# Expert w2 loads begun by ScalarE after the expert's first product, in a streaming transformer block on one core

## The chip, the cores and the metric

The kernel runs on one core of a Trainium2 chip. The metric is the device time of one execution in microseconds (us). It is given as the median of three runs.

## The reference

One block of a hybrid encoder over 256 tokens of width 1024, in float32: RMSNorm, one input projection, sparse attention with an indexer, a pooling mixer, gates, an output projection, and a mixture of 32 experts of which each token uses 4. The part that matters here is the last:

```python
def _moe(h, router_w, router_b, w1, b1, w2, b2):      # w1 (32, 1024, 2048), w2 (32, 1024, 1024), float32
    tok = h.reshape(-1, D_)                             # 256 tokens
    logits = tok @ router_w + router_b
    topv, topi = lax.top_k(logits, 4)
    topw = jax.nn.softmax(topv, axis=-1)
    combine = sum(one_hot(topi, 32) * topw[..., None], axis=1)
    for e in range(32):
        gu = tok @ w1[e] + b1[e]
        gate = jnp.minimum(gu[:, :1024], 7.0)
        lin = jnp.clip(gu[:, 1024:], -7.0, 7.0)
        act = (lin + 1) * gate * jax.nn.sigmoid(1.702 * gate)
        out = out + combine[:, e:e + 1] * (act @ w2[e] + b2[e])
```

The weights of one expert are 8 MB (w1) and 4 MB (w2); all 32 are read once from HBM.

## The kernel before, in words

The kernel is written engine by engine, with semaphores by hand, so each engine's order is the order of its code.

**The ring.** The experts' weights pass through a ring of 10 slots in SBUF. A slot holds a chunk of 2048 KB (128 partitions of 4096 float32). w1 of an expert is 4 chunks and w2 is 2, so an expert is 6 chunks and the whole is 192. `w1_chunk` and `w2_chunk` number them in the order w1(0), w1(1), w2(0), w1(2), w2(1), w1(3), w2(2), and so on to w1(31), w2(30), w2(31). Chunk n lies in the slot that chunk n - 10 had.

**Who loads.** SP (SyncE) begins every one of these loads in its own queue, one after the other, in the order of the numbers (`load_w1`, line 404, and `load_w2`, line 408). Before each it waits until the slot is free (`slot_free`): until TensorE has used chunk n - 10. That is the semaphore `gemm1` for an expert's last w1 chunk, `gemm2` for its last w2 chunk, and `chunk_used` for the others. The two chunks of w2(e) take the slots of the first two chunks of w1(e), and w1(e+2) takes those of the last two chunks of w1(e) and of both chunks of w2(e-1). The last chunk of all is loaded in two halves (lines 450 and 451).

**What TensorE does for an expert.** In the loop over e: `up_expert(e+1)` is the first product of expert e+1, with the bias (line 309) and 4 chunks of 16 matmuls (line 319), each chunk behind a wait for its landing. Its last matmul raises `gemm1` to e+2. Then come the gather of the rows of expert e+2 (line 280), `down_expert(e)`, which is the second product of expert e (2 chunks of 16 matmuls, line 334, which raises `gemm2`), the transposes of the activations of e+1 (325) and of the rows of e+2 (296), the scatter of e's result to the tokens (343), and the transposes of the put matrix (301). So w2(e) is first used after the whole first product of expert e+1.

**What ScalarE does for an expert.** The sigmoid (`sigmoid_gate(e+1)`, line 652, which waits for VectorE's clamp at line 870 and through it for `gemm1`), the copy of the gathered rows (`rows_out(e+2)`, 656), the copy of the second product (`out_out(e)`, 668), and two more copies (660, 664). It begins a few small loads in its own queue, all before the experts.

Of the kernel before, what the change touches and what calls it, by code (L numbers as in the profile page):

```python
# [41 lines left out]
def block_kernel(nc, x, attn_norm_g, w_in, q_norm_g, k_norm_g, pool_w, pool_b, pool_scale,  # L42
                 w_branch_attn, w_branch_pool, w_out, ffn_norm_g, router_w, router_b,
                 expert_w1, expert_b1, expert_w2, expert_b2, out):
    _, T, D = x.shape
    HD = q_norm_g.shape[1]
    DA = w_branch_attn.shape[1]
    H = DA // HD
    G = len(POOL_WINDOWS)
    E = router_w.shape[2]  # L50
# [23 lines left out]
    RING = 10  # L74
    CHUNK_N = 4096
    W1_ROWS, W2_ROWS = CHUNK_N // (2 * FE), CHUNK_N // D
    W1_CHUNKS, W2_CHUNKS = KD // W1_ROWS, KD // W2_ROWS
# [3 lines left out]
    with ExitStack() as ctx:  # L81
# [3 lines left out]
        def sem(name):  # L85
            return ctx.enter_context(nc.semaphore(name))
# [5 lines left out]
        def scratch(slot, at, size):  # L92
# [89 lines left out]
        chunk_in = [sem(f"chunk_in{i}") for i in range(RING)]  # L182
# [12 lines left out]
        pick_ok, gathered, hTe_ok, gemm1, gate_ok, sig_ok, half_ok, glu_ok = (  # L195
            sem(n) for n in "pick_ok gathered hTe_ok gemm1 gate_ok sig_ok half_ok glu_ok".split())
# [46 lines left out]
        def w1_chunk(e, c):  # L243

            return c if e == 0 else W1_CHUNKS + (e - 1) * (W1_CHUNKS + W2_CHUNKS) + c

        def w2_chunk(e, c):

            return (e + 1) * (W1_CHUNKS + W2_CHUNKS) + (W1_CHUNKS - W2_CHUNKS if e < E - 1 else -W2_CHUNKS) + c
# [4 lines left out]
        def chunk_slot(n):  # L254
            return ring[:, SLOT_ORDER[n % RING], :]
# [8 lines left out]
        def w2_dram(e, c):  # L264
            rows = W2_ROWS * P
            return expert_w2[0][bass.ds(e, 1), c * rows:(c + 1) * rows, :].rearrange("a (p k) n -> p (a k n)", p=P)
# [107 lines left out]
        def _(sp):  # L374
# [27 lines left out]
            def load_w1(e, c):  # L402
                n = w1_chunk(e, c)
                sp.dma_start(chunk_slot(n), w1_dram(e, c)).then_inc(chunk_in[n % RING], 16)

            def load_w2(e, c):
                n = w2_chunk(e, c)
                sp.dma_start(chunk_slot(n), w2_dram(e, c)).then_inc(chunk_in[n % RING], 16)
# [21 lines left out]
            def slot_free(n):  # L430
                if n in W1_LAST:
                    sp.wait_ge(gemm1, W1_LAST.index(n) + 1)
                elif n in W2_LAST:
                    sp.wait_ge(gemm2, W2_LAST.index(n) + 1)
                else:
                    sp.wait_ge(chunk_used, n + 1 - sum(last < n for last in W1_LAST + W2_LAST))

            for e in range(1, E):
                if e < E - 1:
                    for c in range(W1_CHUNKS):  # L440
                        slot_free(w1_chunk(e + 1, c) - RING)
                        load_w1(e + 1, c)
                for c in range(W2_CHUNKS):
                    slot_free(w2_chunk(e, c) - RING)
                    if (e, c) != (E - 1, W2_CHUNKS - 1):
                        load_w2(e, c)
                        continue
                    n, half = w2_chunk(e, c), CHUNK_N // 2
                    src = w2_dram(e, c)
                    sp.dma_start(chunk_slot(n)[:, 0:half], src[:, 0:half]).then_inc(chunk_in[n % RING], 16)  # L450
                    sp.dma_start(chunk_slot(n)[:, half:CHUNK_N], src[:, half:CHUNK_N]).then_inc(tail_in, 16)
# [56 lines left out]
        def _(act):  # L508
# [141 lines left out]
            def sigmoid_gate(e):  # L650
                act.wait_ge(gate_ok, e + 1)
                nc.scalar.activation(sig_e, gate_e, ACT.Sigmoid, scale=SWIGLU_ALPHA).then_inc(sig_ok, 1)  # L652

            def rows_out(e):
                act.wait_ge(gathered, e)
                nc.scalar.copy(rows_e, ps_gather[:, :]).then_inc(rows_ok, 1)

            def actT_out(e):
                act.wait_ge(actT_ps, e + 1)
                nc.scalar.copy(actT_e, ps_gate[:, :]).then_inc(actT_sb, 1)  # L660

            def putT_out(e):
                act.wait_ge(put_ps, e + 1)
                nc.scalar.copy(putT[:, :], ps_out[:, 0:T]).then_inc(put_sb, 1)

            def out_out(e):
                act.wait_ge(gemm2, e + 1)
                nc.scalar.copy(out_e, ps_out[:, :]).then_inc(out_ok, 1)  # L668
# [5 lines left out]
            for e in range(E - 1):  # L674
                sigmoid_gate(e + 1)
                if e + 2 < E:
                    rows_out(e + 2)
                out_out(e)
                actT_out(e + 1)
                putT_out(e + 1)  # L680
            out_out(E - 1)

            act.wait_ge(s["most_ok"], 1)
# [638 lines left out]
```

## Time and profile before

| | us |
|---|---|
| median of three runs (1145.51 to 1148.51) | 1147.47 |
| the profiled execution's own time | 1149.56 |
| its span, first to last instruction | 1147.8 |
| TensorE busy | 1095.4 (95%) |
| ScalarE busy | 141.5 (12%) |
| issue to landing of a chunk, median | 42.0 |

The span is divided into 40 slices of 28.7 us. The experts begin at about 223 us, with the eighth slice. A busy digit is a share in tenths, and "PEclk" is the clock that was granted to TensorE. For the DMA engines the page gives the share in which the core's 16 engines were busy and the GB/s that they moved. A chunk is 2.097 MB.

### The profile page before, as it was taken

What the parts mean: (1) busy time and instruction counts of PE and PEld (TensorE: products, weight loads), DVE (VectorE), ACT (ScalarE), POOL (GpSimd) and SP (SyncE); (2) the same over time, 40 slices, a digit from 0 to 9 for tenths busy, and PEclk for the clock granted to TensorE, in tenths of its full rate; (3) what the DMA queues carried; (4) which work ended last, traced back from release to release, by engine and by line L of the source; (5) the groups of instructions that cost most, each with busy time, mean ns of one, the idle gap of its engine ahead of it and who ended that gap; (6) DMA issues with size and microseconds to landing.
All of it is one profiled execution on the core that took longest, in us unless ns stands there. A gap on an engine that the chain in (4) does not pass through costs nothing.

```text
span 1147.8 us, 11145 instructions
## 1 busy us (share of the span) xinstructions
PE 1095.4 (95%) x4910; PEld 427.0 (37%) x4910; DVE 197.1 (17%) x498; ACT 141.5 (12%) x287; POOL 15.1 (1%) x35
## 2 busy tenths in 40 slices
PE   7999999999999999999999998999999999999996
PEld 5464544633333333333333332333333333333332
DVE  1630011411111121111111111111111111111111
ACT  2114111310000110001010000000000000000001
POOL 0004000000000000000000000000000000000000
PEclk9999999789999999999999999999999999999999
DMA  9824527579999999999999999999999999999995
GB/s 344 321 101 147 219 74 286 232 305 426 429 428 427 427 428 429 427 426 428 428 427 429 428 428 427 427 428 427 427 428 427 429 428 428 428 428 428 426 428 227
DMA packets 41667, 432.81 MB, mean 377 GB/s; under 512 B 4189, under 2 KB 5745, under 8 KB 16913
## 3 DMA queue, kind: packets, MB, share of 16 engines
q1 hardware_dynamic: 40128, 431.26, 89.8%
q10 hardware_dynamic: 1488, 0.82, 0.3%
q8 instruction: 40, 0.66, 0.2%
q14 instruction: 11, 0.08, 0.0%
HBM read 431.01 MB, written 1.05 MB: 376 GB/s over the span
## 4 chain that ended last, share of the span: by engine, by line
PE 68%; DMA 31%; DVE 0%; issue 0%; ACT 0%; ACTq 0%
DMA ring<-in_expert_w_dram 31%; PE bank L319 25%; PE bank L334 12%; PE bank L955 8%; PE bank L343 4%; PE bank L280 2%; PE bank L1111 2%; PE bank L1091 2%; PE bank L309 2%; PE bank L325 1%; PE bank L1016 1%; PE bank L296 1%; PE bank L301 1%; PE bank L945 1%; PE bank L289 1%; PE bank L1038 0%
## 5 line engine op out<-in xcount | busy, mean ns | idle before, releaser
L319 PE MATMUL bank<-ring,work 128*64 128x512 f32 x2048 | 454.0, 598 | 17.8 <-DMA ring<-in_expert_w_dram 17.1
L319 PEld LDWEIGHTS bank<-ring,work 128*64 128x64 f32 x2048 | 143.4, 138 | 326.4 <-issue 285.9
L334 PE MATMUL bank<-ring,work 128*64 128x512 f32 x1024 | 230.5, 598 | 19.4 <-DMA ring<-in_expert_w_dram 18.9
L334 PEld LDWEIGHTS bank<-ring,work 128*64 128x64 f32 x1024 | 73.2, 137 | 171.0 <-issue 137.3
L870 DVE TENSOR_SCALAR work<-bank 128x512 f32<-128x512 f32 x32 | 22.1, 692 | 485.7 <-PE bank L319 468.5
L955 PE MATMUL bank<-ring 128*128 128x512 f32 x224 | 98.5, 594 | 0.0
L652 ACT ACTIVATE work<-work 128x512 f32<-128x512 f32 x32 | 20.2, 630 | 499.8 <-DVE work L870 499.8
L343 PE MATMUL bank<-work,putT 64*128 64x512 f32 x256 | 63.6, 615 | 0.7 <-ACT work L668 0.7
L365 DVE TENSOR_TENSOR work<-bank,vecs 128x512 f32<-128x512 f32 x32 | 22.1, 692 | 232.8 <-PE bank L296 230.8
L955 PEld LDWEIGHTS bank<-ring 128*128 128x128 f32 x224 | 41.8, 190 | 48.4 <-issue 48.2
L280 PE MATMUL bank<-xn,pick 128*64 128x512 f32 x248 | 58.5, 592 | 0.0
L668 ACT COPY work<-bank 128x512 f32<-128x512 f32 x32 | 18.8, 587 | 225.5 <-PE bank L334 225.5
L309 PE MATMUL bank<-b_rows,bias_pick 32*64 32x512 f32 x256 | 35.7, 627 | 0.0
L280 PEld LDWEIGHTS bank<-xn,pick 128*64 128x64 f32 x248 | 17.7, 137 | 35.0 <-issue 35.0
L343 PEld LDWEIGHTS bank<-work,putT 64*128 64x128 f32 x256 | 22.0, 186 | 20.5 <-issue 15.1
L1111 PE MATMUL bank<-ring,xn 128*128 128x512 f32 x64 | 28.4, 593 | 0.0
L325 PEld LDWEIGHTS bank<-ident,work 128*128 128x128 f32 x128 | 18.1, 210 | 26.6 <-issue 26.6
L356 DVE TENSOR_SCALAR put<-slot_id,place,weight 128x128 f32<-128x128 f32 x64 | 19.3, 344 | 38.5 <-PE bank L301 38.5
L325 PE MATMUL bank<-ident,work 128*128 128x128 f32 x128 | 24.3, 314 | 0.0
L874 DVE SCALAR_TENSOR_TENSOR work<-work 128x512 f32<-128x512 f32 x32 | 22.2, 693 | 3.7 <-DVE work L871 0.5
L878 DVE TENSOR_TENSOR work<-work 128x512 f32<-128x512 f32 x32 | 22.2, 692 | 1.4 <-ACT work L652 0.4
L871 DVE TENSOR_SCALAR work<-bank 128x512 f32<-128x512 f32 x32 | 21.8, 681 | 0.0
(181 smaller groups left out, 454.6 us busy)
## 6 DMA issues: line engine op xcount, KB each, us to landing
ring<-in_expert_w_dram SPq DMA_DIRECT2D x191, 2048.0 KB, 42.0
ring<-in_w_in_dram SPq DMA_DIRECT2D x8, 2048.0 KB, 19.9
ring<-in_w_out_dram SPq DMA_DIRECT2D x2, 2048.0 KB, 7.9
ring<-in_w_branch_attn_dram SPq DMA_DIRECT2D x1, 2048.0 KB, 7.9
ring<-in_w_branch_pool_dram SPq DMA_DIRECT2D x1, 2048.0 KB, 7.9
ring<-in_expert_w_dram SPq DMA_DIRECT2D x2, 1024.0 KB, 43.8
ring<-in_w_in_dram SPq DMA_DIRECT2D x1, 1296.0 KB, 8.1
xs<-in_x_dram SPq DMA_DIRECT2D x2, 512.0 KB, 4.5
```

The lines of the kernel that those rows point to most:

```text
L280: mm = pe.matmul(ps_gather[SLOTS * half:SLOTS * (half + 1), :], pick[:, tt, :], xn[:, tt, half * BANK:(half + 1) * BANK], start=(tt == 0), ...
L309: mm = pe.matmul(dst, bias_pick[rows, :], b1_rows[rows, :], start=first, stop=not first, skip_group_check=True)
L319: mm = pe.matmul(dst, hTe[:, at:at + SLOTS], w[:, col:col + BANK], start=(k == 0 and not bias_first), stop=(k == KD - 1 and bias_first), s ...
L325: mm = pe.transpose(ps_gate[:, j * P:(j + 1) * P], every(act_e, W2_ROWS, j), ident[:, :])
L334: mm = pe.matmul(ps_out[SLOTS * half:SLOTS * (half + 1), :], actT_e[:, at:at + SLOTS], w[:, col:col + BANK], start=(k == 0), stop=(k == KD ...
L343: mm = pe.matmul(acc[2 * tt + half][:, :], putT[rows, tt * P:(tt + 1) * P], out_e[rows, :], start=False, stop=True, skip_group_check=True)
L365: return nc.vector.tensor_tensor(hTe.rearrange("p (j h n) -> p j h n", j=4, h=2), ps_gather[:, :].rearrange("p (j h n) -> p j h n", j=4, h ...
L874: nc.vector.scalar_tensor_tensor(out=lin_e, in0=lin_e, scalar=1.0, in1=gate_e, op0=ALU.add, op1=ALU.mult).then_inc(half_ok, 1)
L878: nc.vector.tensor_tensor(act_e, lin_e, sig_e, ALU.mult).then_inc(glu_ok, 1)
L955: mm = pe.matmul(dst, hT[:, k, tt * P:(tt + 1) * P], w[:, k, :], start=(k == 0), stop=(k == KD - 1))
L1091: mm = pe.matmul(bank[2 + 2 * (j % 2) + n][:, :], src[:, k, tt * P:(tt + 1) * P], w[:, k, half * BANK:(half + 1) * BANK], start=(k == 0), ...
L1111: mm = pe.matmul(bank[2 * tt + half][:, :], mergedT[tt][:, k, :], w[:, k % 4, half * BANK:(half + 1) * BANK], start=(k == 0), stop=(k == K ...
```

## The change

SP no longer loads w2 of the experts 1 to 30. ScalarE begins these loads in its own queue: after the sigmoid of expert e+1 it waits for `gemm1` of that expert, which means until all four w1 chunks of e+1 are used, and starts both w2 chunks of e+1. Then it goes on with the copy of the gathered rows. SP still loads all of w1, w2(0) and w2(31). The slots and the chunks' semaphores are the same.

```diff
--- before.py
+++ after.py
@@ -440,7 +440,7 @@
                     for c in range(W1_CHUNKS):
                         slot_free(w1_chunk(e + 1, c) - RING)
                         load_w1(e + 1, c)
-                for c in range(W2_CHUNKS):
+                for c in range(W2_CHUNKS if e == E - 1 else 0):
                     slot_free(w2_chunk(e, c) - RING)
                     if (e, c) != (E - 1, W2_CHUNKS - 1):
                         load_w2(e, c)
@@ -663,6 +663,13 @@
                 act.wait_ge(put_ps, e + 1)
                 nc.scalar.copy(putT[:, :], ps_out[:, 0:T]).then_inc(put_sb, 1)
 
+            def load_w2(e):
+
+                act.wait_ge(gemm1, e + 1)
+                for c in range(W2_CHUNKS):
+                    n = w2_chunk(e, c)
+                    act.dma_start(chunk_slot(n), w2_dram(e, c)).then_inc(chunk_in[n % RING], 16)
+
             def out_out(e):
                 act.wait_ge(gemm2, e + 1)
                 nc.scalar.copy(out_e, ps_out[:, :]).then_inc(out_ok, 1)
@@ -674,6 +681,7 @@
             for e in range(E - 1):
                 sigmoid_gate(e + 1)
                 if e + 2 < E:
+                    load_w2(e + 1)
                     rows_out(e + 2)
                 out_out(e)
                 actT_out(e + 1)
```

SP's queue at the experts 0 and 1, before. Of these rows the `x3` and the `gemm1` behind it are w1(2), the next row is w2(1), the four after it are w1(3), and the last is w2(2):

```order
L408 DMA ring<-in_expert_w2_dram 128x4096
L404 DMA ring<-in_expert_w1_dram 128x4096 [waits chunk_used] x3
L404 DMA ring<-in_expert_w1_dram 128x4096 [waits gemm1]
L408 DMA ring<-in_expert_w2_dram 128x4096 [waits chunk_used] x2
L404 DMA ring<-in_expert_w1_dram 128x4096 [waits chunk_used]
L404 DMA ring<-in_expert_w1_dram 128x4096 [waits gemm1]
L404 DMA ring<-in_expert_w1_dram 128x4096 [waits chunk_used]
L404 DMA ring<-in_expert_w1_dram 128x4096 [waits gemm2]
L408 DMA ring<-in_expert_w2_dram 128x4096 [waits chunk_used] x2
```

The same place now:

```order
L408 DMA ring<-in_expert_w2_dram 128x4096
L404 DMA ring<-in_expert_w1_dram 128x4096 [waits chunk_used] x3
L404 DMA ring<-in_expert_w1_dram 128x4096 [waits gemm1]
L404 DMA ring<-in_expert_w1_dram 128x4096 [waits chunk_used]
L404 DMA ring<-in_expert_w1_dram 128x4096 [waits gemm1]
L404 DMA ring<-in_expert_w1_dram 128x4096 [waits chunk_used]
L404 DMA ring<-in_expert_w1_dram 128x4096 [waits gemm2]
```

After w1(2), SP goes straight to w1(3), whose first chunk waits for the third chunk of w1(1) to be used. Before, the two chunks of w2(1) came between them, behind the first and second chunk of w1(1).

ScalarE's order at expert 1 (first row: its sigmoid), before:

```order
L652 ACTIVATE work<-work 128x512 [waits gate_ok]
L656 COPY work<-bank7 128x512 [waits gathered]
L668 COPY work<-bank6 128x512 [waits gemm2]
L660 COPY work<-bank4 128x512 [waits actT_ps]
L664 COPY putT<-bank6 128x256 [waits put_ps]
```

And now (line 675 is the former 668):

```order
L652 ACTIVATE work<-work 128x512 [waits gate_ok]
L671 DMA ring<-in_expert_w2_dram 128x4096 [waits gemm1]
L671 DMA ring<-in_expert_w2_dram 128x4096
L656 COPY work<-bank7 128x512 [waits gathered]
L675 COPY work<-bank6 128x512 [waits gemm2]
L660 COPY work<-bank4 128x512 [waits actT_ps]
L664 COPY putT<-bank6 128x256 [waits put_ps]
```

The two loads stand between the sigmoid and the copy of the gathered rows.

## Rows read from the trace of the kernel before

**Rows 1.** Page, part 2: TensorE and DMA busy in 40 slices, in tenths.

```profile
PE   7999999999999999999999998999999999999996
DMA  9824527579999999999999999999999999999995
```

**Rows 2.** Stretches: length, busy PE, PEld, DVE, ACT, POOL; then PEclk, DMA share, GB/s.

```profile
10.00:15.00 5.00, 3.72 (x19) 3.20 (x18) 1.15 (x2) 1.83 (x7) 0.00 (x0) 1.00 1.05 387
15.00:20.00 5.00, 5.00 (x25) 4.21 (x24) 0.00 (x0) 0.58 (x1) 0.00 (x0) 1.00 1.07 386
...
235.00:243.00 8.00, 8.00 (x43) 2.36 (x39) 1.79 (x3) 1.68 (x3) 0.00 (x0) 1.00 1.00 430
249.00:256.00 7.00, 7.00 (x29) 1.97 (x29) 1.53 (x5) 0.32 (x1) 0.00 (x0) 0.72 0.29 122
285.00:600.00 315.00, 315.00 (x1522) 111.45 (x1520) 52.06 (x118) 32.78 (x59) 0.00 (x0) 1.00 1.01 428
```

**Rows 3.** Waits from 600 to 1136 us: us in total, times, longest.

```profile
PE bank L334 <- DMA ring<-in_expert_w_dram: 18.9, 17, 2.4
PE bank L319 <- DMA ring<-in_expert_w_dram: 17.1, 17, 1.2
```

**Rows 4.** Timeline of SP's loads, neighbours merged: start, us to the last's end.

```profile
255.86 3.76 SPq L408 DMA_DIRECT2D ring<-in_expert_w_dram  x2
262.73 12.34 SPq L404 DMA_DIRECT2D ring<-in_expert_w_dram  x4
282.79 3.76 SPq L408 DMA_DIRECT2D ring<-in_expert_w_dram  x2
289.65 12.34 SPq L404 DMA_DIRECT2D ring<-in_expert_w_dram  x4
...
1090.76 2.65 SPq L451 DMA_DIRECT2D ring<-in_expert_w_dram  x1
```

**Rows 5.** Issue to landing of the load at 255.86, then of the last.

```profile
DMA to landing us min/median/max: 8.1/8.1/8.1
...
DMA to landing us min/median/max: 44.8/44.8/44.8
```

**Rows 6.** TensorE's timeline: the second product of expert 1 begins.

```profile
294.59 1.89 PE L334 MATMUL bank<-ring,work 128*64 128x512 f32 x8
```

**Rows 7.** TensorE's timeline at the end: start, us, idle before it.

```profile
1116.06 3.65 PE L319 MATMUL bank<-ring,work 128*64 128x512 f32 x16 [1.01 <-DMA ring<-in_expert_w_dram]
1121.05 3.65 PE L334 MATMUL bank<-ring,work 128*64 128x512 f32 x16 [1.34 <-DMA ring<-in_expert_w_dram]
1125.85 3.65 PE L334 MATMUL bank<-ring,work 128*64 128x512 f32 x16 [1.14 <-DMA ring<-in_expert_w_dram]
...
1133.05 7.09 PE L334 MATMUL bank<-ring,work 128*64 128x512 f32 x32 [0.51 <-issue]
1140.82 1.99 PE L343 MATMUL bank<-work,putT 64*128 64x512 f32 x8 [0.68 <-ACT work L668]
```

**Rows 8.** Page, part 6: loads in ScalarE's queue and SP's; KB, us to landing.

```profile
pool_wsb<-in_pool_w_dram ACTq DMA_DIRECT2D x1, 256.0 KB, 11.1
ring<-in_w_in_dram SPq DMA_DIRECT2D x8, 2048.0 KB, 19.9
```

**Rows 9.** ScalarE: a load of its queue, then its work in one expert.

```profile
16.35 0.45 ACTq L540 DMA_DIRECT2D pool_wsb<-in_pool_w_dram  x1
...
854.68 0.63 ACT L652 ACTIVATE work<-work 128x512 f32<-128x512 f32 x1 [16.49 <-DVE work L870]
855.67 0.59 ACT L656 COPY work<-bank 128x512 f32<-128x512 f32 x1 [0.36 <-PE bank L280]
863.76 0.59 ACT L668 COPY work<-bank 128x512 f32<-128x512 f32 x1 [7.50 <-PE bank L334]
```

**Rows 10.** TensorE after its longest wait among the experts, and the clock there.

```profile
713.16 5.35 PE L334 MATMUL bank<-ring,work 128*64 128x512 f32 x16 [2.45 <-DMA ring<-in_expert_w_dram]
...
714.00:719.00 5.00, 5.00 (x18) 1.69 (x15) 0.00 (x0) 0.44 (x1) 0.00 (x0) 0.68 1.03 439
```

## The prediction, made before the changed kernel ran

> **What bounds the kernel now.** I read the two strips of the page first. TensorE is busy nearly everywhere, and so are the DMA engines from the tenth slice on [rows 1]. That both are near full doesn't say which one sets the pace, so the second view is the table of stretches: from 285 us on the DMA engines move 428 GB/s without a gap (a share of 1.01) [rows 2]. A chunk of 2.097 MB thus takes 2.097 / 428 = 4.90 us, and an expert's six take 29.4 us. The third view is SP's timeline. The w2 loads of two experts running begin at 255.86 and 282.79 us, so TensorE, which frees the slots, needs 26.93 us for an expert when it doesn't wait [rows 4]. TensorE is the faster of the two by 2.46 us an expert. It first lives on the chunks that are loaded ahead, and then waits: from 600 us on 18.9 us before chunks of w2 and 17.1 us before chunks of w1 [rows 3]. The DMA stream is the bound. It has run without a break since the load at 255.86 us: that chunk lands 8.1 us after its issue, at 264.0, the other 177 follow at 4.90, which gives 1131, and the last one lands at 1090.76 + 44.8 = 1135.6 us [rows 4, 5]. The 4.3 us between are small gaps of 0.5% in all, which I leave as they are. The end is then set by two things alone: when this stream begins and whether it breaks, and how much TensorE work hangs on its last chunks.
>
> Right before the stream there is a hole. From 249 to 256 us the DMA share is 0.29 [rows 2]: w1(2) is loaded and SP waits for the first chunk of w1(1) to be used.
>
> **The change part by part.**
>
> *The start of the stream.* Before, the hole ends with w2(1) at 255.86 us. Now SP's next load is w1(3,0), which waits for the third chunk of w1(1). In the trace it goes out at 262.73 us [rows 4], and nothing delays TensorE before that, so it will again. ScalarE's w2(1) comes later still, after the fourth chunk. The hole grows by 262.73 - 255.86 = 6.87 us. From 262.73 to about 275 us all six loads of this round are begun; they last 29.4 us, to 292, and the next load (w1(4,0)) goes out at 289.65 us [rows 4]. So the stream does not break again, and each later round has 2.46 us more in hand. The last chunk lands 6.9 us later, at 1142.5 us. **Term 1: +6.9 us.**
>
> Does TensorE feel the hole at once? w2(1) is begun at about 268 us and needed at 294.59 us [rows 6]. At half the rate, two chunks take 4 x 4.90 = 19.6 us and land by about 291 us with the fixed part of 8.1 - 4.90 = 3.2 us. There are 4 us to spare. This costs nothing by itself.
>
> *The order at the end.* Now as the queue stands, four chunks come behind w1(31,3): both of w2(30) and both of w2(31). 1116.06 + 4 x 4.90 = 1135.7 us, which is where the last one lands [rows 5, 7]. With the change w2(30) is begun right after the first product of expert 30. That is one round (29.4 us) before the first product of expert 31 ends. Two queues then want the same engines. If they get half each, w2(30) is in after 19.6 us (and 3.2), before w1(31,3), which it has pushed back. Behind w1(31,3) there is only w2(31), 9.8 us. So w1(31,3) lands at 1142.5 - 9.8 = 1132.7 us instead of 1116.0. This is 6.9 us from term 1, and two chunks' time on top. **Term 2: +9.8 us.** The bytes are the same; what is worse is that the chunk on which most of the remaining TensorE work hangs now comes later in the stream.
>
> *What follows w1(31,3).* Before, it is 1140.82 + 1.99 - 1116.06 = 26.75 us to the end of the scatter, and this holds two waits for w2(30), of 1.34 and 1.14 us [rows 7]. Now w2(30) has landed, and these go. **Term 3: -2.5 us.** What is late next? The second product of expert 31 then starts 1133.05 - 1116.06 - 2.48 = 14.5 us behind 1132.7, at 1147.2 us, when w2(31) has been in for almost 5 us. Nothing else takes their place.
>
> *The middle.* The stream stays the bound: 29.4 us against 26.93. The waits of 36 us move to another place, one wait of about 2.5 us an expert at the last w1 chunks, none at w2. That alone costs nothing. It has a side effect, though. The longest wait of before, 2.45 us, is followed by 16 matmuls in 5.35 us instead of 3.65, with the granted clock at 0.68 over that stretch, that is, partly at 1.2 GHz instead of 2.4 [rows 7, 10]. If every wait of 2.5 us does this, TensorE needs 26.93 + 1.7 = 28.6 us an expert, still under 29.4, so the middle hides it. Before the last product it is not hidden: 0 to +1.7 us. I take half. **Term 4: +0.8 us.**
>
> *What ScalarE pays.* Two issues of about 0.45 us [rows 9] in each of 30 experts, 27 us in all. They stand between the sigmoid, which ends at 855.31, and the copy of the rows at 855.67 us. Behind that copy ScalarE is idle for 7.50 us, and TensorE wants the copied rows only after the second product, about 7 us later [rows 9, 7]. A copy that is 0.6 us later is covered. SP's last issue took 2.65 us [rows 4]; two of these would make 5 us, still within the 7. Cost 0; what the cover would have to lose is 7 us. SP's 60 fewer issues gain nothing, since SP waits anyway.
>
> *The rate with two queues at once.* No row of before shows two queues full of 2048 KB loads. The nearest are the first loads: 387 GB/s in 10 to 15 us with SP's queue alone, 386 in 15 to 20 us with ScalarE's beside it, in smaller packets [rows 2]. And ScalarE's 256 KB are in after 11.1 us beside SP's queue, whose 2048 KB blocks need 19.9 [rows 8], so one queue doesn't wait for the other to be empty. The gain is bounded by 439 GB/s, the highest figure in any row, over 5 us [rows 10]: 2.5% of the 872 us of stream, -22 us. The same distance down, 417 GB/s, would be +22 us. I take 0, by the nearest row, 386 against 387, and keep about 1% to either side for the range.
>
> The Trainium skill (DMA: Bandwidth & Descriptors, "Issuing engines are not separate DMA queues") says that loads issued by different engines run on the same 16 DMA engines and interleave, and that a second issuer saves only issue time. It speaks against any gain, and by it the sum is the one above. The same page ("Bandwidth") gives 435 GB/s as the ceiling of the fabric; a stream at that figure would be an estimated 1.6% or 14 us shorter, which would just cancel the sum. The trace has 430 GB/s over 8 us of such loads, and 439 only over 5 us [rows 2, 10].
>
> **The sum.** +6.9 + 9.8 - 2.5 + 0.8 = +15.0 us. The span goes from 1147.8 to 1162.8, the profiled execution's time from 1149.56 to 1164.6. That execution lies 2.1 us above the median of 1147.47, so for the median I say 1162.5 us, +1.3%.
>
> **The rivals.**
>
> *A. The stream gets faster with two queues (the other side).* While one queue is between two packets, the other one fills the engine. For it: a granted share of 16 engines says little about gaps inside a packet, and overlap holds in 4 of 6 chunks. Against: 386 beside 387. At 434 GB/s, halfway to the bound of 439, the price is -12, the sum +3, the time 1150; it decides from 4.82 us a chunk on, where the 14 to 15 us are won back. At the bound it is 1141. Chance 0.11.
>
> *B. The engines serve the loads in the order of issue.* Then w2(30) doesn't push ahead. At the end it is issued behind w1(31) and w2(31), and lands last, at 1142.5 us. From the landing of the second w2(30) chunk to the end it was 1140.82 + 1.99 - 1125.85 = 16.96 us [rows 7]: 1159.5 against 1142.8, +16.7, the time 1164. Rows 8 speak against it. Chance 0.08.
>
> *C. The stream gets slower.* Two streams from different places of HBM disturb each other by 1%: +9, the time 1171 (at the bound of 417, 1185). For it: nothing but that it's untried. Chance 0.09.
>
> *D. ScalarE's queue gets less than a third.* Below that, 2 x 4.90 x 3 = 29.4 us is a whole round, and w2 comes late for every second product. At 0.3 it is 32.7 us, 3.3 late, of which 2.5 are idle anyway: 0.8 x 30 = 24, with term 1 some +31, the time 1178. Chance 0.04.
>
> The forecast has the remaining 0.68.
>
> **How the numbers follow.** Against 1147.47, 0.3% is 3.4 us, about what a measurement of this kernel can tell from no change. Faster needs 1144 or less, which only the far end of A gives: 0.04. Same is the middle of A: 0.05. Its near end (1151 to 1155), the forecast and B, C, D are slower: 0.91. The forecast's own range is 1158 to 1166 (term 4, the rate by 0.4%). For 8 in 10 I add B and most of C, and the nearer end of A: 1154 to 1172.
>
> **What would show it.** Right: the hole before the stream ends at about 262.7 us instead of 255.9, with the first ScalarE load near 268; the last chunk lands near 1142 us; the waits for DMA at the second product are gone, and one of 2 to 3 us stands before the last w1 chunk in each later expert; some of them with a lower clock behind; w2 loads land some 20 to 23 us after issue, where all loads needed 42; GB/s stays at 428. Wrong: GB/s of 432 or more (A) or 424 or less (C); waits before the second product (B, D); a hole in the DMA strip past 300 us.

## The result, and the profile after

| | before | changed |
|---|---|---|
| median of 4 runs, us | 1147.99 | 1160.98 |
| lowest to highest | 1145.51 to 1148.52 | 1159.12 to 1161.85 |
| profiled execution's own time | 1149.56 | 1159.12 |
| its span | 1147.8 | 1157.3 |

The ratio is 1.0118, 95% interval 1.0104 to 1.0131: slower by 13 us. A second set, taken later (below), gave 1.0129, 1.01 to 1.0158.

The strips of the changed kernel's page, as in [rows 1]:

```profile
PE   7999999999999999989999999999999989999997
DMA  9823517569999999999999999999999999999993
```

They look like those of before. What differs is too small for a digit of 29 us. The stretches of the changed kernel, with the columns of [rows 2]:

```profile
249.00:256.00 7.00, 7.00 (x34) 2.30 (x32) 0.00 (x0) 0.00 (x0) 0.00 (x0) 1.00 0.06 23
256.00:262.00 6.00, 6.00 (x30) 2.01 (x28) 0.20 (x1) 0.00 (x0) 0.00 (x0) 1.00 0.45 134
...
285.00:600.00 315.00, 304.33 (x1448) 105.95 (x1446) 48.37 (x110) 30.34 (x55) 0.00 (x0) 0.99 1.01 428
600.00:900.00 300.00, 284.50 (x1324) 98.25 (x1322) 46.58 (x105) 28.81 (x52) 0.00 (x0) 0.98 1.01 428
900.00:1100.00 200.00, 189.66 (x888) 65.23 (x886) 28.19 (x67) 18.09 (x33) 0.00 (x0) 0.97 1.01 427
```

From 249 to 256 us the DMA share fell from 0.29 to 0.06: the hole is wider. The figures of this one stretch can't be compared exactly, since w1(2) came in somewhat earlier here (the clock, below); the run that gives w2 of 1 to 3 back to SP measures the hole alone. Behind it stands the same rate of 427 to 428 GB/s, now with two queues. The clock's column goes down from 1.00 to 0.97 towards the end.

The issues around the hole (start, us to the last one's end):

```profile
258.36 3.76 SPq L404 DMA_DIRECT2D ring<-in_expert_w_dram  x2
262.54 0.84 ACTq L671 DMA_DIRECT2D ring<-in_expert_w_dram  x2
```

The last load's second half (duration in ns, start), with the time from issue to landing of both halves:

```profile
L451 SPq DMA_DIRECT2D ring<-in_expert_w_dram x1: 433/433/433, 1103.1 to 1103.1; - x1
DMA to landing us min/median/max: 32.9/34.0/35.0
```

The stream begins at 258.36 us and its last part lands at 1103.1 + 35.0 = 1138.1: 879.7 us. Before it was 1135.6 - 255.86 = 879.7 us [rows 4, 5]. To a tenth of a microsecond the same bytes take the same time.

The groups of loads on the page, with KB and median us to landing, beside the 42.0 of before:

```profile
ring<-in_expert_w_dram SPq DMA_DIRECT2D x131, 2048.0 KB, 36.4
ring<-in_expert_w_dram ACTq DMA_DIRECT2D x60, 2048.0 KB, 19.5
```

The 19.5 us is the middle between two kinds of loads and no load's own time. The two loads of a pair stand one behind the other in ScalarE's queue. Over all 60 of them, and over the first pair, issued at 262.54 and 262.92 us, the times to landing are:

```profile
DMA to landing us min/median/max: 13.7/19.5/25.1
...
DMA to landing us min/median/max: 15.8/20.4/25.1
```

The first load of a pair lands 13.7 to 15.8 us after its issue, the second 23.2 to 25.1 us. The second lands a median of 9.8 us behind the first. That is 2 x 4.90 us for one chunk: half the rate, while SP's queue has the other half. And the waits for loads from 600 to 1136 us, where [rows 3] had two lines:

```profile
PEld bank L319 <- DMA ring<-in_expert_w_dram: 43.3, 18, 4.6
PE bank L319 <- DMA ring<-in_expert_w_dram: 28.0, 17, 3.7
```

The line of the second product (L334) is gone. All waiting is now before w1. The end of TensorE's timeline, to be laid beside [rows 7]:

```profile
1115.63 10.52 PE L319 MATMUL bank<-ring,work 128*64 128x512 f32 x48
1128.36 3.65 PE L319 MATMUL bank<-ring,work 128*64 128x512 f32 x16 [2.21 <-DMA ring<-in_expert_w_dram]
1131.85 7.04 PE L334 MATMUL bank<-ring,work 128*64 128x512 f32 x32
...
1142.43 7.09 PE L334 MATMUL bank<-ring,work 128*64 128x512 f32 x32 [0.51 <-issue]
1150.19 1.99 PE L343 MATMUL bank<-work,putT 64*128 64x512 f32 x8 [0.68 <-ACT work L675]
```

w1(31,3) lands at 1128.4 us, 9.8 us before the last chunk and no longer 19.6. From there to the end of the scatter it is 1150.19 + 1.99 - 1128.36 = 23.8 us without one wait for a load, against 26.75.

The two profiled executions differ by 9.5 us, the medians by 13. The traces show one reason: the clock just before the stream. In the profile of before TensorE began the first product of expert 1 later:

```profile
251.40 4.85 PE L319 MATMUL bank<-ring,work 128*64 128x512 f32 x18
```

In the changed kernel's profile:

```profile
247.80 13.95 PE L319 MATMUL bank<-ring,work 128*64 128x512 f32 x64
```

Before, the clock was at 0.72 over the stretch from 249 to 256 us [rows 2], and here it was at 1.00. What the profiled before lost there, 3.6 us, and the 0.8 us of the product's slower start hide 4.4 of the 6.9 us of the first term in a comparison of the two traces: 258.36 - 255.86 = 2.5 us, and 2.5 + 9.8 - 2.9 = 9.4 us of span. Other executions weren't traced, but among 17 of the kernel before that were timed beside one group of the runs below, the 4 with a mean granted clock of 0.989 over the execution, which the profiled one had too, took 1151.1 to 1151.6 us, and the 13 with 0.993 to 0.996 took 1145.2 to 1148.7 us.

### The profile page after: what moved, and what is told of

Same layout as the page of the kernel before. It is cut to its first block, busy times and chain, and to the rows that moved or that the text cites. A ratio compares the mean times of both kernels' runs of the same rounds, so it can differ in the third digit from the quotient of the medians.

```text
span 1157.3 us, 11145 instructions
## 1 busy us (share of the span) xinstructions
PE 1102.0 (95%) x4910; PEld 428.9 (37%) x4910; DVE 197.0 (17%) x498; ACT 141.3 (12%) x287; POOL 15.1 (1%) x35
## 4 chain that ended last, share of the span: by engine, by line
PE 51%; DMA 48%; DVE 0%; issue 0%; ACT 0%; ACTq 0%
DMA ring<-in_expert_w_dram 48%; PE bank L319 14%; PE bank L334 12%; PE bank L963 8%; PE bank L280 3%; PE bank L1119 2%; PE bank L1099 2%; PE bank L343 1%; PE bank L1024 1%; PE bank L309 1%; PE bank L953 1%; PE bank L289 0%; PE bank L325 0%; PE bank L1046 0%; DMA xs<-in_x_dram 0%; PE bank L942 0%
## 5 line engine op out<-in xcount | busy, mean ns | idle before, releaser
L319 PE MATMUL bank<-ring,work 128*64 128x512 f32 x2048 | 468.7, 613 | 39.5 <-DMA ring<-in_expert_w_dram 38.7
L319 PEld LDWEIGHTS bank<-ring,work 128*64 128x64 f32 x2048 | 145.9, 141 | 358.8 <-issue 297.1
L334 PE MATMUL bank<-ring,work 128*64 128x512 f32 x1024 | 225.2, 592 | 0.5 <-issue 0.5
L334 PEld LDWEIGHTS bank<-ring,work 128*64 128x64 f32 x1024 | 73.7, 137 | 146.1 <-issue 146.1
L675 ACT COPY work<-bank 128x512 f32<-128x512 f32 x32 | 18.7, 586 | 199.4 <-PE bank L334 199.4
## 6 DMA issues: line engine op xcount, KB each, us to landing
ring<-in_expert_w_dram SPq DMA_DIRECT2D x131, 2048.0 KB, 36.4
ring<-in_expert_w_dram ACTq DMA_DIRECT2D x60, 2048.0 KB, 19.5
ring<-in_w_in_dram SPq DMA_DIRECT2D x8, 2048.0 KB, 19.5
```

What stands on the lines that cost most here:

```text
L319: mm = pe.matmul(dst, hTe[:, at:at + SLOTS], w[:, col:col + BANK], start=(k == 0 and not bias_first), stop=(k == KD - 1 and bias_first), s ...
L334: mm = pe.matmul(ps_out[SLOTS * half:SLOTS * (half + 1), :], actT_e[:, at:at + SLOTS], w[:, col:col + BANK], start=(k == 0), stop=(k == KD ...
```

## The experiments

All were timed in three groups, on three chips, each group beside runs of the kernel before on the same chip. The groups are the runs that give back w2 of 1 to 3, of 30, and of both, with the changed kernel again; then w2 of 1 alone, one queue, ScalarE's early issue, and the better kernel; then the two runs over three rounds at the end. Where a number of microseconds against before is given, it is the ratio's distance from 1 times 1147. In the expectations T is the theory of the prediction, with terms 1 to 3. Q blames ScalarE's queue, and C here blames TensorE's clock (it isn't the prediction's rival C).

### Undo the start: SP loads w2 of the experts 1 to 3

```diff
-                for c in range(W2_CHUNKS if e == E - 1 else 0):
+                for c in range(W2_CHUNKS if e <= 3 or e == E - 1 else 0):
...
-                    load_w2(e + 1)
+                    if e + 1 > 3:
+                        load_w2(e + 1)
```

> SP loads w2 of the experts 1 to 3 again, in its old order; ScalarE begins those of 4 to 30. Theory T (the loss is a later start of the stream, +6.9 us, and w2(30) ahead of w1(31), +9.8 - 2.5 us; measured sum +13): the hole at 250 us is as before, and by expert 4 the DMA engines are 3 x 2.46 = 7.4 us behind TensorE, enough to cover the later issue. So the first term goes: +6 us against the kernel before (5 to 8). Rival Q (each load in ScalarE's queue, or two queues at once, costs something, 13 us over 30 experts): 27/30 of it stays, +11.7 us. Rival C (the falls of TensorE's clock cost it): they stay, +13 us.

Measured: 1152.92 us, ratio 1.006 (1.0037 to 1.0084), +6.9 us. The loads of 27 of 30 experts are still ScalarE's and half of the loss is gone. Theory T fits; Q's +11.7 lies outside the interval (4.2 to 9.6 us), and so does C's +13: in the same trace TensorE still waits 30.0 us for loads before w1, and none before w2, and the mean granted clock is 0.982, where the changed kernel's is 0.980 in its trace of the same group.

```profile
PEld bank L319 <- DMA ring<-in_expert_w_dram: 45.0, 17, 4.0
PE bank L319 <- DMA ring<-in_expert_w_dram: 30.0, 17, 3.1
```

The two traces of that group also give term 1 by itself, since TensorE reached this place at the same time in both (w1(1)'s product starts at 247.89 and 247.74 us). The first load behind the hole, here and in the changed kernel:

```profile
251.58 0.33 SPq L408 DMA_DIRECT2D ring<-in_expert_w_dram  x1
...
258.30 0.33 SPq L404 DMA_DIRECT2D ring<-in_expert_w_dram  x1
```

The hole ends 6.7 us later with the change; term 1 says 6.9.

### Undo it for expert 1 alone

```diff
-                for c in range(W2_CHUNKS if e == E - 1 else 0):
+                for c in range(W2_CHUNKS if e == 1 or e == E - 1 else 0):
...
-                    load_w2(e + 1)
+                    if e + 1 > 1:
+                        load_w2(e + 1)
```

> SP loads w2(1) again, ScalarE those of 2 to 30. T: the first stream begins at 255.86 us as before, but its six chunks are through after 29.4 us, and the next load, w1(4,0), goes out only at 289.65 us. A new hole of 289.65 - 255.86 - 29.4 = 4.4 us opens one round later; only 2.5 us of the 6.9 are won back: +10.5 us against the kernel before (9 to 12), with a hole in the DMA share near 290 us. Rival S (only the load at the first hole matters): 6.9 us are won, +6 us.

Measured: 1160.33 us, ratio 1.0106 (1.0083 to 1.0128), +12.2 us, just above the 9 to 12 expected; S's +6 is out (interval 9.5 to 14.7 us). The time alone can't tell this kernel from the changed one; the trace can. The second hole is there. The stretches of this kernel:

```profile
249.00:256.00 7.00, 7.00 (x38) 2.21 (x32) 1.04 (x5) 0.00 (x0) 0.00 (x0) 1.00 0.60 204
256.00:262.00 6.00, 6.00 (x32) 2.01 (x28) 0.00 (x0) 0.00 (x0) 0.00 (x0) 1.00 1.00 429
280.00:290.00 10.00, 10.00 (x48) 3.30 (x46) 0.00 (x0) 0.00 (x0) 0.00 (x0) 1.00 0.63 236
```

The first hole closes early (share 0.60 where the changed kernel has 0.06). But from 280 to 290 us the share is 0.63, a hole of 3.7 us (4.4 expected). From the first issue behind the first hole to the last landing the stream takes 884.4 us in this trace instead of 879.7, so the second hole costs 4.7 us. The hole was moved by one round, and only some 2 us of it were closed.

### Undo the end: SP loads w2(30)

```diff
-                for c in range(W2_CHUNKS if e == E - 1 else 0):
+                for c in range(W2_CHUNKS if e >= E - 2 else 0):
...
-                    load_w2(e + 1)
+                    if e + 1 < E - 2:
+                        load_w2(e + 1)
```

> SP loads w2(30) again, behind w1(31); ScalarE begins those of 1 to 29. T: behind w1(31,3) there are again four chunks, it lands two chunks earlier, and the waits before w2(30) come back: 9.8 - 2.5 = 7.3 us less than the changed kernel, +5 to +7 us against the kernel before. Q: 29/30 stays, +12.6 us. C: +13 us.

Measured: 1158.77 us, ratio 1.01 (1.008 to 1.0119), +11.5 us. This was a miss: T said +5 to +7. Neither do Q (+12.6) and C fall by this run alone. TensorE's timeline of this kernel shows why:

```profile
1101.36 5.35 PE L319 MATMUL bank<-ring,work 128*64 128x512 f32 x16 [2.20 <-DMA ring<-in_expert_w_dram]
...
1119.69 13.95 PE L319 MATMUL bank<-ring,work 128*64 128x512 f32 x64
1133.47 7.04 PE L334 MATMUL bank<-ring,work 128*64 128x512 f32 x32
```

The last wait for a load is at w1(30,3), which had w2(29) ahead of it as in the changed kernel. After that all 64 matmuls of expert 31's first product run through without a wait, so w1(31) had been there in time. It was of no use, because TensorE itself was one reordering late, and it gains only 29.4 - 26.93 = 2.5 us on the loads in a round.

The clock took part of even that. The 16 matmuls behind the wait took 5.35 us instead of 3.65, at a granted clock of 0.72 from 1101 to 1107 us. At the same place the changed kernel's profile has

```profile
1099.00 3.65 PE L319 MATMUL bank<-ring,work 128*64 128x512 f32 x16 [0.58 <-DMA ring<-in_expert_w_dram]
```

From there to the second product of expert 30 it is 1131.85 - 1099.00 = 32.9 us in the changed kernel and 1133.47 - 1101.36 = 32.1 us here: 0.7 us are gained in this profiled execution, about the 2.5 us less 1.7 us for the slow matmuls. No wait follows in which those could hide.

### Both at once, with only expert 30 at the end

SP loads w2 of 1 to 3 and of 30:

```diff
-                for c in range(W2_CHUNKS if e == E - 1 else 0):
+                for c in range(W2_CHUNKS if e <= 3 or e >= E - 2 else 0):
...
-                    load_w2(e + 1)
+                    if 3 < e + 1 < E - 2:
+                        load_w2(e + 1)
```

> Both: SP loads w2 of 1 to 3 and of 30, ScalarE those of 4 to 29. T: both terms go, 0 us against the kernel before (-1.5 to +1.5), though 26 experts still use two queues, the waits still stand before w1, and the clock still falls. Q: 26/30 stays, +11.3 us. C: +13 us less the share of experts with falls that is gone, above +10 us.

Measured: 1150.87 us, ratio 1.003 (1.0017 to 1.0043), +3.4 us. Q and C are out by far: 26 of 30 experts run as in the changed kernel. But T's 0 is missed too (interval 1.9 to 4.9 us). What the run above was short of is about 5 us: the 7.3 us of the end less the 2.5 us that one round gives back, 4.8. Of this 3.4 us show here. In the profile it is 4.8: behind the last landing, at 1130.4 us, the kernel runs 17.0 us to its end, against 12.2 us in the profile of before.

### The changed kernel again, on the same chip

No edit: it gives the size of the loss on the chip of three of the runs above (w2 of 1 to 3, of 30, and both; w2 of 1 alone was timed on another).

> The changed kernel on the same chip as the three others: +13 us (11.5 to 15) against the kernel before, ratio 1.0118 within 0.002, by every theory.

Measured: 1160.49 us, ratio 1.0129 (1.01 to 1.0158), +14.8 us.

### One queue, the same late moment

```diff
+            for c in range(W1_CHUNKS):
+                next_w1(2, c)
+            for e in range(1, E - 1):
+                if e < E - 2:
+                    next_w1(e + 2, 0)
+                    next_w1(e + 2, 1)
...
+                sp.wait_ge(gemm1, e + 1)
+                for c in range(W2_CHUNKS):
+                    load_w2(e, c)
+                if e < E - 2:
+                    next_w1(e + 2, 2)
+                    next_w1(e + 2, 3)
```

(`next_w1` waits for the slot and loads. For expert 30 the two chunks of w2(31) stand in place of w1's, ahead of w2(30); the lines left out do this, and ScalarE begins no expert's load.)

> No load of ScalarE. SP begins w2(e) itself, at the same moment as the changed kernel does (after gemm1 of e), behind w1(e+2,1) and ahead of w1(e+2,2), all in one queue; at the end w2(30) stands behind w2(31). T: the start is late by 6.9 us as in the changed kernel, and in one queue w2(30) now lands last, so that 16.96 us of TensorE work follow the last chunk: 2.5 us more than the changed kernel, +14 to +17 us against the kernel before; w2 lands about 35 us or more after issue instead of 19.5. Q (ScalarE's queue is the cost): the cost goes, 0 to +7 us.

Measured: 1165.45 us, ratio 1.0163 (1.0142 to 1.0184), +18.7 us (16.3 to 21.1), a little over T's range. ScalarE's queue is not what costs: without it the loss is all there, and Q's 0 to +7 is out. In the two profiles the stream begins at 264.31 us here and at 255.86 before, 8.45 us later and 1.6 more than term 1; the clock before it was lower still, 0.60 from 249 to 256 us. w2 loads land after 31.4 us (median), the two of a pair 4.9 us apart instead of 9.8, and the end of TensorE's timeline has the two waits before w2(30) again, behind which all the rest hangs:

```profile
1123.11 13.95 PE L319 MATMUL bank<-ring,work 128*64 128x512 f32 x64
1139.75 3.65 PE L334 MATMUL bank<-ring,work 128*64 128x512 f32 x16 [2.69 <-DMA ring<-in_expert_w_dram]
1144.52 3.65 PE L334 MATMUL bank<-ring,work 128*64 128x512 f32 x16 [1.12 <-DMA ring<-in_expert_w_dram]
```

### ScalarE's queue, the old moment

```diff
             def load_w2(e):
 
-                act.wait_ge(gemm1, e + 1)
                 for c in range(W2_CHUNKS):
                     n = w2_chunk(e, c)
+                    act.wait_ge(chunk_used, n - RING + 1 - sum(last < n - RING for last in W1_LAST + W2_LAST))
...
             for e in range(E - 1):
+                if e + 2 < E:
+                    load_w2(e + 1)
                 sigmoid_gate(e + 1)
                 if e + 2 < E:
-                    load_w2(e + 1)
                     rows_out(e + 2)
```

> ScalarE begins w2 of 1 to 30 in its own queue, but at the moment at which SP did in the kernel before: chunk by chunk, when the slot is free, ahead of the sigmoid. T: the first term goes (no longer hole), the order at the end stays as in the changed kernel or a little earlier: 9.8 - 2.5 = +7.3 us, +6 to +8 us against the kernel before. Q: all 60 loads are in ScalarE's queue, +13 us. A rival S2 (the second queue is harmless and only the late issue costs): 0 us.

Measured: 1155.37 us, ratio 1.0068 (1.0048 to 1.0088), +7.8 us. Both Q (13) and S2 (0) are out. The first issue is at 255.72 us, so the hole is that of before, and what is left is the order at the end. It isn't quite the end that T had in mind. The lines of this profile:

```profile
1099.96 5.02 PE L319 MATMUL bank<-ring,work 128*64 128x512 f32 x16 [4.36 <-DMA ring<-in_expert_w_dram]
...
1117.96 13.95 PE L319 MATMUL bank<-ring,work 128*64 128x512 f32 x64
```

The last wait is before w1(30,3), as in the run with w2(30) given back, and w1(31) is there in time. In the kernel before the same matmuls began at 1086.70 us. Both streams begin within 0.2 us of each other and both end at 1135.6 to 1135.7 us, so w1(30,3) is 13.3 us late by order alone, and TensorE makes up for a part of it. So T's +7.3 fits by its size, and not by the chunk that it named. The second queue isn't harmless, but not because it is a queue: half the rate goes to the loads that aren't due yet.

### Undo the end over three rounds

SP loads w2 of 28 to 30:

```diff
-                for c in range(W2_CHUNKS if e == E - 1 else 0):
+                for c in range(W2_CHUNKS if e >= E - 4 else 0):
...
-                    load_w2(e + 1)
+                    if e + 1 < E - 4:
+                        load_w2(e + 1)
```

> SP loads w2 of the experts 28 to 30, ScalarE those of 1 to 27. The run that gave only w2(30) back to SP kept 11.5 us of the loss, and in its trace the first product of expert 31 ran without any wait for a load: TensorE itself was late there, since w1(30) had still landed behind w2(29), and it wins back only 29.4 - 26.93 = 2.5 us an expert. Theory T, mended: the order has to be undone over three rounds (3 x 2.5 = 7.4 us) for the end to come back. Expected: 9.8 - 2.5 = 7.3 us less than the changed kernel, +5.5 to +7.5 us against the kernel before. Rival Q (cost per load of ScalarE's queue): 27/30 of the loss, about +13 us. Rival E (the order at the end was never worth more than the 2 to 3 us of that run): +11 us.

Measured: 1154.08 us, ratio 1.0049 (1.0032 to 1.0066), +5.6 us. Q and E are out.

### Both, over three rounds each

```diff
-                for c in range(W2_CHUNKS if e == E - 1 else 0):
+                for c in range(W2_CHUNKS if e <= 3 or e >= E - 4 else 0):
...
-                    load_w2(e + 1)
+                    if 3 < e + 1 < E - 4:
+                        load_w2(e + 1)
```

> SP loads w2 of 1 to 3 and 28 to 30, ScalarE those of the 24 experts between, late as in the changed kernel. T, mended: both terms are gone, -1 to +1 us against the kernel before, though the middle is wholly the changed kernel's (two queues, late issues, falls of the clock). Q: 24/30 of the loss, about +11 us. E: +3 us, like the run with only w2(30).

Measured: 1147.84 us, ratio 1.0003 (0.9985 to 1.0021), +0.3 us. 24 of the 30 experts run with the change, and no cost of it is left (interval -1.7 to +2.4 us); E's +3 is out too. The stretch of this kernel from 400 to 900 us, and the end of its TensorE timeline:

```profile
400.00:900.00 500.00, 478.07 (x2247) 165.52 (x2243) 75.03 (x172) 46.95 (x85) 0.00 (x0) 0.98 1.01 427
```

```profile
1104.95 13.95 PE L319 MATMUL bank<-ring,work 128*64 128x512 f32 x64
1118.73 3.60 PE L334 MATMUL bank<-ring,work 128*64 128x512 f32 x16
1122.56 3.65 PE L334 MATMUL bank<-ring,work 128*64 128x512 f32 x16 [0.23 <-DMA ring<-in_expert_w_dram]
```

The clock stays at 0.98 in the middle, as in the changed kernel, at no cost that shows. At the end a wait stands before w2(30) again (0.23 us), the sign that TensorE has just caught up with the loads.

### A better kernel: begin the stream earlier

The same reasoning shortens the hole of the kernel before. It ends when w1(1,0) is used. Ahead of that TensorE runs eight matmuls that start the accumulators with b2.

```diff
-            for j in range(2 * TT):
+            for j in range(0, 2 * TT, 2):
                 start_acc(j)
...
                 if e + 2 < E:
                     gather_expert(e + 2)
+                if e == 0:
+                    for j in range(1, 2 * TT, 2):
+                        start_acc(j)
                 down_expert(e)
```

> The kernel before, all loads in SP's queue, but two of the four groups of matmuls that start the accumulators with b2 (line 1147) run after the first product of expert 1 instead of ahead of it. They are half of 3.7 to 4.4 us. T says that the hole at 250 us ends when the first chunk of w1(1) is used and that the whole stream hangs on it: 1.8 to 2.2 us earlier, -2 us against the kernel before (-3 to -1). A theory in which TensorE's total work or the DMA bytes alone set the time says 0.

Measured: 1144.07 us, ratio 0.9974 (0.996 to 0.9987), -3.0 us, faster than both. Only half of the matmuls can move, since the other half's b2 lies where the activations' transposes of expert 0 go. Its timeline around the place:

```profile
241.67 1.98 PE L1147 MATMUL bank<-work,pool_wsb 32*128 32x512 f32 x4
...
246.12 13.95 PE L319 MATMUL bank<-ring,work 128*64 128x512 f32 x64
259.90 1.89 PE L280 MATMUL bank<-xn,pick 128*64 128x512 f32 x8
261.72 1.98 PE L1147 MATMUL bank<-work,pool_wsb 32*128 32x512 f32 x4
```

TensorE does the same work, 1.98 us of it 20 us later, and the kernel is shorter by 3.0 us (1.5 to 4.6). The first product of expert 1 begins at 246.12 us; in the changed kernel, which has the old order here, it began at 247.80. That is 1.7 us, in two profiles with the full clock at this place. What goes beyond it may be the clock again, which is granted in full from 242 to 262 us here and stood at 0.83 in the profile of before. Whether moving the matmuls also keeps the clock up isn't shown.

## Why the prediction was right

The forecast was 1162.5 us, and 1160.98 was measured. By its steps:

- *The bound.* Right. 879.7 us of stream in both profiles; 427 to 428 GB/s in every long stretch.
- *Term 1, the later start, +6.9.* Right. Giving w2 of 1 to 3 back to SP took 14.8 - 6.9 = 7.9 us off on the same chip, and in the two traces of that group the stream begins 6.7 us apart. In the profiles of before and after only 2.5 us show, since the clock had been low at that place in the profiled before. The prediction's words that nothing delays TensorE before that, so that it will be the same again, were wrong: that clock did. I read the 262.73 us of the first SP load from that one execution; in the changed one it was 258.36. The difference of the two issues (6.87 us, two chunks of matmuls) held, the absolute times did not.
- *Term 2, the order at the end, +9.8, and term 3, -2.5.* Right: 9.8 us from w1(31,3) to the last landing, and 23.8 instead of 26.75 us behind it, so -2.9. Early issue in ScalarE's queue (+7.8) and giving back 28 to 30 (14.8 - 5.6 = 9.2 us off, on two chips) each frame the 7.3 us within their intervals. For the early issue the trace has another chunk late than the one that the term names, w1(30,3) and not w1(31,3). And at most 2.5 us of the 9.8 come back by putting right the last round alone.
- *Term 4, the clock, +0.8.* Half right. The clock does fall behind longer waits in the middle. In the changed kernel's profile, one of those:

```profile
508.53 5.35 PE L319 MATMUL bank<-ring,work 128*64 128x512 f32 x16 [3.69 <-DMA ring<-in_expert_w_dram]
```

  It costs nothing there. It did cost 1.7 us in the run with only w2(30) given back, where it fell behind the last wait of all. At the end of the changed kernel's profile the last 16 matmuls of the first product took 3.65 us, so the term was 0 in the profiled run. This accounts for 0.8 of the 1.5 us by which the forecast was too high, as far as one execution can tell.
- *ScalarE's cost, 0.* Right: two issues in 0.84 us, and none of TensorE's waits is for ScalarE in the middle.
- *The rate with two queues, 0.* Right: 427 to 428 GB/s. Rivals A and C fall with it. The rule of the Trainium skill that I quoted (DMA: Bandwidth & Descriptors, "Issuing engines are not separate DMA queues") agrees with this trace: the two loads of a pair landed 9.8 us apart instead of 4.9, interleaved with SP's, and no bandwidth came of the second queue.
- *Rival B, service in the order of issue.* Wrong for two queues: all 60 of ScalarE's loads landed within 25.1 us, while SP's, some of them issued earlier, took 36.4. In one queue it is what happens: +18.7 us where the rival's sum had +16.7.
- *Rival D, under a third.* The shares were halves, and the forecast rested on that. Its sum for a pair, 19.6 us and 3.2, was a little short: the second load was in 24.4 us after its issue (median). The first pair was in at 288.0 us, and TensorE began the second product of expert 1 at 290.24.

There was some luck in the level. The forecast for the profiled execution was 1164.6 us, and 1159.12 was measured: 4.4 of these 5.5 us are the clock before the stream, low in the profile that I read and full in the new one. The 2.1 us that I took off to get to the median probably stood, unknown to me, for a part of the same thing, so the forecast of the median came closer than that of the profile.

What I had not seen is that the loss is kept by TensorE, not by the loads. It wins back 2.5 us a round at most. So either end has to be undone over three rounds. I reckoned with that at the start of the stream, and overlooked it at the end, where the run with only w2(30) given back was expected at +5 to +7 and came out at +11.5. The two ratios of the changed kernel stand for 13.5 and 14.8 us. Differences of a microsecond or two between single results stay open. What makes the clock low before the stream in some executions stays open too.

## What to carry to other kernels

In this kernel, whose loads stream without a break, neither a second queue nor a later issue changed the bandwidth. In such a case look at when the stream starts, where it breaks, and how much compute hangs on its last loads. Two queues of equal loads shared by halves here, so loads that are due later must not get a queue of their own beside those that are due next. Delays that vanish in the middle of a long loop can be paid in full at both ends, and an engine that needs only 8% less time than its loads takes several rounds to make up for one reordering.

## What the runs showed of the hardware

Two queues of equal 2048 KB loads divided the engines evenly: the two loads of a pair landed 9.8 us apart in ScalarE's queue beside SP's loads, and 4.9 us apart in one queue, with 427 to 428 GB/s in sum either way. A load at the head of ScalarE's queue was in after 14 us, while SP's took 36.4.

The granted clock can stay at 0.97 to 0.98 over hundreds of microseconds, as it falls behind single waits, without any effect that shows where the loads are the bound: 16 matmuls that take 3.65 us at 2.4 GHz took 5.35 with a part of them at 1.2. Behind the last wait the same fall costs its 1.7 us in full. The length of the wait didn't decide it: 2.21 us before 1128.36 us in the changed kernel brought no fall, and 2.20 us before 1101.36 us in the run with w2(30) given back did.
